# An expert stage in which each pair of experts gathers its own token rows

## The chip, the cores and the metric

The kernel runs on one core of a Trainium2 chip. The metric is device time in microseconds, the median of several executions; the profile is one execution of its own. Engines are named PE (TensorE), DVE (VectorE), ACT (ScalarE), POOL (GpSimd) and SP (SyncE, which here only issues transfers).

## What is computed

Two transformer blocks over 512 tokens of width 1024, all in float32. The first mixes a convolution with latent attention and ends in a mixture of experts; the second has two layers of sliding-window and sparse attention with a dense feed-forward part. The change is in the mixture of experts and in the add behind it:

```
g_idx = top_1(softmax(h @ w_group))                   # 4 groups
e_idx = top_2(softmax(h @ w_expert in that group))    # 8 experts each, 32 in all
gates[token, expert] = g_top * e_top / sum(e_top)     # two experts a token
for e in range(32):
    a = silu(h @ w_gate_e[e]) * (h @ w_up_e[e])       # 1024 -> 256
    y += gates[:, e] * (a @ w_down_e[e])              # 256 -> 1024
x = x + g_f * y
```

h is the second norm of x with scale and shift. Each token goes to two of 32 experts, so there are 1024 (token, expert) rows, 32 an expert on average.

## The kernel before

Everything is written by hand, with a program for each engine and semaphores between them; an engine does its work in the order of its program.

**Routing.** POOL makes ramps and constants (lines 977 to 983), then the rstd of the second norm (987, 988), for which DVE waits at line 1641. PE turns the normed rows (L2145), makes the logits (L2292), and counts with matmuls how many tokens before each chose the same expert (L2300 to L2303). DVE makes prefix sums of the counts, and from them for every row a place in a list sorted by expert. PE turns the places into a list of token numbers with a one-hot product (L2310, "rows"), and in the same way into a list of target rows ("slots"). POOL then gathers all 1024 sorted rows with eight indirect transfers (L993) out of token_rows, a copy of the normed rows in HBM. PE turns them in 64 pieces of 128x128, and ACT (L1210) and DVE (L1780) apply scale and shift as they empty PSUM in 512 columns, into XsT.

**The loop.** The 32 experts go in 16 pairs (EPAIRS). Each expert has a window of 64 columns (HALF) beginning at its first row. DVE copies the two windows of a pair out of XsT into XW (`window`, L1790), two pairs ahead. PE multiplies them with gate and up weights, the experts side by side in PSUM bank b = p % 2 (L2339, 16 matmuls, 32 in the trace); ACT takes SiLU (L1215), DVE the product (L1795), PE turns it (L2327), ACT copies it (L1219), PE makes the down product (L2356) into two banks of bank b's own pair, DVE (L1799) and ACT (L1223) copy a half each to Y, and POOL scatters the rows to expert_rows in HBM (L1002). The sequence on PE is gate/up of p, turn, down of p, gate/up of p + 1.

**The weights.** SP loads them ahead: 2.1 MB of gate and up for an expert into one of five slots (L830), 1.05 MB of down into one of four (L833), each when the product that last used the slot is done (m_gu, m_y).

**The extra steps.** An expert with more than 64 rows needs further windows of 128. How many there are is read from a register, at least one step is run, and here it is one. It stands behind the last pair on all engines, and loads its weights in the same rings.

**Behind the loop.** SP reads expert_rows back (L872), two rows a token. ACT weights one (L1248), DVE the other and adds (L1857), multiplies by g_f (L1858) and adds to x (L1861); then the second block begins with its input projection (L2398 turns, L2410 products with w_in).

## Time and profile before

| | us |
|---|---|
| three runs | 2058.57, 2051.89, 2056.76 |
| median | 2056.76 |
| the profiled execution | 2054.31, its span 2052.5 |
| PE busy in the span | 1844.0 (90%) |
| DVE, ACT, POOL busy | 915.1, 622.2, 162.3 |
| mean DMA rate | 132 GB/s, 270.38 MB |

The page gives a span in 40 slices of 51 us. The expert stage is slices 7 to 13, from 328 us, where the constants of the routing are made, to 650 us, where the rows are read back. The slices show where the transfers are dense; the timelines give start and duration of each instruction, and behind it in brackets how long the engine had been idle and what it waited for. Durations of matmuls overlap a little, since they are pipelined.

### The profile page before, as it was taken

The page shows a single profiled execution, that of the slowest core. Times are in us where ns is not written, and L with a number is a line of the kernel's source. Part 1 is how long each engine was busy: PE and PEld are TensorE (multiplying, and loading weights), DVE is VectorE, ACT ScalarE, POOL GpSimd, SP SyncE. Part 2 cuts the span into 40 slices and gives each one's busy share as a digit, 9 for nine tenths or more (in the row PEclk, how much of TensorE's full clock was granted, in tenths as well). Part 3 has the DMA queues.
Part 4 walks back from the last instruction along what each step waited for, and adds up shares of the span by engine and source line. Part 5 has one row for each costly group of instructions (what it writes and reads, how often), then busy time and mean ns, then how long its engine had stood idle before and what let it go on. Part 6 is the DMA issues. An engine that isn't in the chain of part 4 may idle for free. (4 is left out here: it accounts for less than half of the span.)

```text
span 2052.5 us, 23756 instructions
## 1 busy us (share of the span) xinstructions
PE 1844.0 (90%) x8688; PEld 1262.0 (61%) x8692; DVE 915.1 (45%) x1646; ACT 622.2 (30%) x1121; POOL 162.3 (8%) x239
## 2 busy tenths in 40 slices
PE   4997996587776899999999999988999999999996
PEld 2444644423222556676788878865557678888785
DVE  3787823511102687682322223347866522222234
ACT  2024521110001225742333322223376223333222
POOL 1000000200000242010000000004500100000001
PEclk9999998799888899999999999999999999999998
DMA  9162034499995500032233342250002203334231
GB/s 377 75 246 83 1 126 164 176 420 421 421 422 199 207 1 13 10 119 57 62 102 89 95 143 82 86 196 1 1 22 114 62 23 100 102 94 151 72 93 42
DMA packets 146334, 270.38 MB, mean 132 GB/s; under 512 B 9344, under 2 KB 106624, under 8 KB 132672
## 3 DMA queue, kind: packets, MB, share of 16 engines
q1 hardware_dynamic: 142208, 259.44, 34.9%
q0 software_dynamic: 4032, 9.69, 1.3%
q8 instruction: 58, 0.95, 0.2%
q14 instruction: 36, 0.29, 0.0%
HBM read 260.72 MB, written 13.11 MB: 133 GB/s over the span
## 5 line engine op out<-in xcount | busy, mean ns | idle before, releaser
L278 PE MATMUL bank<-ht_hi,gate_up_hi 128*128 128x512 f32 x704 | 274.1, 389 | 3.1 <-ACT arena L1429 3.1
L280 PE MATMUL bank<-ht_hi,gate_up_lo 128*128 128x512 f32 x704 | 273.9, 389 | 0.0
L279 PE MATMUL bank<-ht_lo,gate_up_hi 128*128 128x512 f32 x704 | 273.9, 389 | 0.0
L2410 PE MATMUL bank<-arena 128*128 128x512 f32 (+3 forms) x640 | 197.1, 467 | 8.2 <-ACT arena L1276 5.6
L2410 PEld LDWEIGHTS bank<-arena 128*128 128x128 f32 x640 | 115.3, 197 | 84.6 <-issue 67.4
L2054 DVE TENSOR_TENSOR arena<-arena,bank 128x512 f32 (+1 forms) x44 | 30.2, 687 | 272.2 <-ACT arena L1295 272.2
L278 PEld LDWEIGHTS bank<-ht_hi,gate_up_hi 128*128 128x128 f32 x704 | 132.1, 188 | 31.3 <-issue 3.9
L280 PEld LDWEIGHTS bank<-ht_hi,gate_up_lo 128*128 128x128 f32 x704 | 132.1, 188 | 27.7
L279 PEld LDWEIGHTS bank<-ht_lo,gate_up_hi 128*128 128x128 f32 x704 | 132.1, 188 | 27.2
L278 PE MATMUL bank<-down_hi,product_hi 128*128 128x512 f32 x352 | 138.2, 393 | 3.5 <-DVE arena L2054 3.5
L280 PE MATMUL bank<-down_hi,product_lo 128*128 128x512 f32 x352 | 138.1, 392 | 0.0
L279 PE MATMUL bank<-down_lo,product_hi 128*128 128x512 f32 x352 | 138.0, 392 | 0.0
L2048 DVE TENSOR_TENSOR gate_up_lo<-gate_up_whole,gate_up_hi 128x2048 fp32r<-128x2048 f32 x44 | 100.9, 2293 | 67.5 <-ACT gate_up_hi L1289 66.9
L2058 DVE TENSOR_TENSOR down_lo<-down_whole,down_hi 128x1024 fp32r<-128x1024 f32 x44 | 53.9, 1225 | 157.7 <-ACT product_hi L1303 157.7
L2339 PE MATMUL bank<-arena 128*64 128x512 f32 x512 | 113.0, 593 | 8.1 <-DMA arena<-w_up_e 4.0
L1301 ACT CAST down_hi<-down_whole 128x1024 fp32r<-128x1024 f32 x44 | 46.2, 1051 | 164.2 <-PE bank L280 164.2
L2356 PE MATMUL bank<-arena 128*64 128x512 f32 x256 | 73.7, 728 | 20.4 <-DMA arena<-w_down_e 16.9
L1514 DVE SCALAR_TENSOR_TENSOR arena<-arena 128x512 f32<-128x512 f32 x120 | 90.0, 750 | 3.3
L2339 PEld LDWEIGHTS bank<-arena 128*64 128x64 f32 x512 | 40.4, 137 | 78.5 <-issue 78.3
L1289 ACT CAST gate_up_hi<-gate_up_whole 128x2048 fp32r<-128x2048 f32 x44 | 84.0, 1908 | 0.2
L2145 PE MATMUL bank<-arena 128*128 128x128 f32 (+1 forms) x332 | 54.1, 318 | 29.9 <-DVE arena L1575 11.8
L1295 ACT ACTIVATE arena<-bank 128x512 f32<-128x512 f32 x44 | 26.3, 598 | 174.4 <-PE bank L280 174.2
(373 smaller groups left out, 2938.0 us busy)
## 6 DMA issues: line engine op xcount, KB each, us to landing
gate_up_whole<-w_gu SPq DMA_DIRECT2D x88, 512.0 KB, 5.1
arena<-w_gate_e SPq DMA_DIRECT2D x33, 1024.0 KB, 20.1
arena<-w_up_e SPq DMA_DIRECT2D x33, 1024.0 KB, 23.4
arena<-w_down_e SPq DMA_DIRECT2D x33, 1024.0 KB, 23.2
down_whole<-w_down SPq DMA_DIRECT2D x44, 512.0 KB, 3.5
arena<-w_ada SPq DMA_DIRECT2D x5, 4096.0 KB, 21.2
arena<-w_in SPq DMA_DIRECT2D x4, 2048.0 KB, 16.0
w_o_whole<-w_o SPq DMA_DIRECT2D x2, 4096.0 KB, 13.1
```

Source lines behind the costliest of these rows:

```text
L278: pe.matmul(ps, xh, wh, start=start, stop=False)
L279: pe.matmul(ps, xh, wl, start=False, stop=False)
L280: return pe.matmul(ps, xl, wh, start=False, stop=stop)
L1289: act.copy(gu_hi[s], gu[s]).then_inc(f_hi, 1)
L1301: act.copy(dn_hi[f % 2], w_dn[:, f % DN_SLOTS])
L1514: ins = dve.scalar_tensor_tensor(DW[:, m], U[:, m, k:k + S], conv_w[:, m, k:k + 1], DW[:, m], ALU.mult, ALU.add)
L2048: dve.tensor_tensor(gu_lo[s], gu[s], gu_hi[s].bitcast(F32), ALU.subtract).then_inc(f_lo, 1)
L2058: dve.tensor_tensor(dn_lo[f % 2], w_dn[:, f % DN_SLOTS], dn_hi[f % 2].bitcast(F32), ALU.subtract)
L2145: ins = pe.transpose(ps[0:x.shape[-1], n * P:(n + 1) * P], x, ident)
L2339: ins = pe.matmul(bank[b][half_rows(h)], XW[b][:, c, half_rows(h)], ring[gu_slot(2 * p + h)][:, :, c], start=c == 0, stop=c == C8 - 1)
L2356: ins = pe.matmul(bank[4 + 2 * b + half][half_rows(h)], AT[:, b, c, half_rows(h)], ring_d[dn_slot(2 * p + h)][:, c, 512 * half:512 * half ...
L2410: ins = pe.matmul(ps[:, 0:b - a], HT[:, c, t * P:(t + 1) * P], w_in2[j][:, c], start=c == 0, stop=c == C8 - 1)
```

## The change

**Places.** There are no sorted rows any more. An expert's slots are fixed, 64 e to 64 e + 63, and one table gives for every slot the token to read, the row to write and the weight of the row (`mark_places`, `take_table`; from_token, to_row, w_slot). The first table, for the 16 pairs, is made before the loop. The counting of extra steps and their table (`extra_rows`) stand on DVE between the first pair's product and the gating of its rows, and their matmuls on PE behind the second pair's gate/up product.

**Rows.** Pair p gathers its own 128 rows with one indirect transfer into G[p % 2], skipping empty slots; POOL issues the gather of p + 1 behind the scatter of p - 1. PE turns them in eight pieces (`turn_rows`, L2340) into banks 6 and 7, ACT and DVE apply scale and shift in four pieces of 128 columns each (`modulate`), into XT. On PE the down product of pair p stands ahead of the turns of pair p + 1. The down product has one pair of banks, 4 and 5, instead of two.

**Weights of the rows.** DVE multiplies the weight into the product (L1765) and g_f into the rows as it empties PSUM (`gate_rows`, both halves; L1771), so that behind the loop only the add is left.

**Slots and extras.** A sixth gate/up slot and a fifth down slot are filled before the loop and then used by the extra steps, which stand before pair 9. POOL makes two more ramps and clears G before the rstd.

```diff
-XCOLS = 2 * S + P
 HALF = P // 2
 EPAIRS = NE // 2
-COLUMNS = 32
-EXTRAS = COLUMNS - EPAIRS
+EXTRAS = NE - EPAIRS
+EXTRA_AT = 9
+XCOLS = EXTRAS + 1
 ARENA = 53200
 CREDIT = 4
-GU_SLOT, DN_RING = [2, 3, 0, 1, 4], 4
-GU_USES_EXTRA, DN_USES_EXTRA = NE // len(GU_SLOT), NE // DN_RING
-GU_AT_EXTRA, DN_AT_EXTRA = (NE - len(GU_SLOT)) // 2, (NE - DN_RING) // 2
+EXTRA_STEPS = 11
+GU_SLOT = [2, 3, 0, 1, 4, 5] + [[2, 3, 0, 1, 4][n % 5] for n in range(NE - 6)]
+DN_SLOT = [0, 1, 2, 3, 4] + [n % 4 for n in range(NE - 5)]
+GU_EXTRA, DN_EXTRA = 5, 4
+ABSENT = 4096
...
+            for e in (0, 1, 4):
+                load_down(e, DN_SLOT[e])
             u1.read(sp, ("mix", T - 1, 1))
-            load_gate_up(2, gu_slot(2))
-            load_gate_up(3, gu_slot(3))
+            load_gate_up(2, GU_SLOT[2])
+            load_gate_up(3, GU_SLOT[3])
             for t in range(T):
                 sp.wait_ge(s_xhat2, t + 1)
                 sp.dma_start(token_rows[t * P:(t + 1) * P], H[:, t]).then_inc(s_saved, 16)
             for e in range(2, 4):
-                load_down(e, dn_slot(e))
-            u1.all_evacuated(sp, [("xsT", g, c) for g in range(2) for c in range(C8)])
-            load_gate_up(4, gu_slot(4))
+                load_down(e, DN_SLOT[e])
+            load_gate_up(4, GU_SLOT[4])
+            sp.wait_ge(s_saved, 16 * T)
+            u1.read(sp, ("logit", T - 1))
+            load_gate_up(5, GU_SLOT[5])
...
-            sp.wait_ge(s_extra, 1)
-            extras = sp.value_load(n_extra[0:1, 0:1], min_val=1, max_val=EXTRAS)
-            with sp.Fori(0, extras) as x:
-                e = sp.value_load(extra_i[0:1, 0, bass.ds(x, 1)], min_val=0, max_val=NE - 1)
-                sp.wait_ge(m_gfree, x + 1)
-                load_gate_up(e, gu_slot(NE))
-                sp.wait_ge(m_dfree, x + 1)
-                load_down(e, dn_slot(NE))
-            sp.wait_ge(m_st[0], 16 * (EPAIRS // 2 + extras))
...
+            own.mark(pool.iota(column_h, [[1, P]], base=0, channel_multiplier=0, allow_small_or_imprecise_dtypes=True))
+            own.mark(pool.iota(slot_h, [[HALF, NE]], base=0, channel_multiplier=0, allow_small_or_imprecise_dtypes=True))
             own.mark(pool.tensor_copy(ones_b, ones))
             own.mark(pool.tensor_copy(before_b, before_me))
+            own.settle()
+            own.mark(pool.tensor_scalar(column_h, column_h, 0.5 - HALF, None, ALU.add))
+            own.mark(pool.tensor_scalar(slot_h, slot_h, 0.5 - HALF, None, ALU.add))
+            for b in range(2):
+                own.mark(pool.memset(G[b], 0.0))
             own.settle()
             pool.sem_inc(s_count, 1)
...
-            u1.evacuated(pool, ("rows",))
-            for g in range(2):
-                for q in range(T):
-                    pool.indirect_dma_start(stage[g][:, q], None, token_rows,
-                                            bass.IndirectOffsetOnAxis(row_ids[:, T * g + q:T * g + q + 1], 0)).then_inc(s_stage1 if g else s_stage, 16)
-
-            u1.evacuated(pool, ("slots",))
-            pool.memset(XsT[:, :, 2 * S:], 0.0).then_inc(s_pad, 1)
-            last_row = pool.to_reg(2 * S - 1)
+            last_row, last_token = pool.to_reg(2 * S - 1), pool.to_reg(S - 1)
+
+            def gather(p):
+
+                if p >= 2:
+                    pool.wait_ge(m_xt, p - 1)
+                pool.indirect_dma_start(G[p % 2], None, token_rows, bass.IndirectOffsetOnAxis(from_token[:, p:p + 1], 0),
+                                        bounds_check=last_token, oob_is_err=False).then_inc(s_g[p % 2], 16)
...
+            pool.wait_ge(s_tokens, 1)
+            gather(0)
+            gather(1)
+            u1.evacuated(pool, ("table",))
+            apart(pool)
             for p in range(EPAIRS):
-                pool.wait_ge(m_ya, p + 1)
-                pool.wait_ge(m_yb, p + 1)
-                pool.indirect_dma_start(expert_rows, bass.IndirectOffsetOnAxis(slots_i[:, p:p + 1], 0), Y[:, p % 2], None,
-                                        bounds_check=last_row, oob_is_err=False).then_inc(m_st[p % 2], 16)
...
+                if p == EXTRA_AT:
+                    pool.wait_ge(s_extra, 2)
+                    apart(pool)
+                    pool.indirect_dma_start(G[2], None, token_rows, bass.IndirectOffsetOnAxis(from_token[:, EPAIRS:EPAIRS + 1], 0),
+                                            bounds_check=last_token, oob_is_err=False).then_inc(s_gx, 16)
+                    scatter(p - 1)
...
+                elif p:
+                    scatter(p - 1)
+                if p + 1 < EPAIRS and p:
+                    gather(p + 1)
+            scatter(EPAIRS - 1)
...
+            def modulate(b):
+
+                for c in range(C8 // 2):
+                    ins = act.activation(XT[b][:, c], bank[6 + c // 4][:, c % 4 * P:(c % 4 + 1) * P], ACT.Identity,
+                                         bias=mod[:, 2, c:c + 1], scale=mod[:, 3, c:c + 1])
+                return ins
+
+            act.wait_ge(m_xt, 1)
+            modulate(0).then_inc(m_xw, 1)
...
+                act.wait_ge(m_gu, p + 1)
                 if p >= 2:
                     act.wait_ge(m_a, p - 1)
-                silu(p, b)
+                silu(b).then_inc(m_silu, 1)
+                act.wait_ge(m_at, p + 1)
                 if p >= 2:
                     act.wait_ge(m_y, p - 1)
-                copy_at(p, b)
-                if p >= 2:
-                    act.wait_ge(m_st[b], 16 * (p // 2))
-                copy_y(p, b)
...
-            def weight_second(t):
-
-                act.wait_ge(s_yin[t], 16)
-                act.activation(Yin[:, t, 1], Yin[:, t, 1], ACT.Copy, scale=wts[:, t, 1:2]).then_inc(s_w1, 1)
-
-            weight_second(0)
-            weight_second(1)
+                copy_at(b).then_inc(m_atc, 1)
+                if p + 1 < EPAIRS:
+                    act.wait_ge(m_xt, p + 2)
+                    modulate(1 - b).then_inc(m_xw, 1)
...
+            def mark_places(n):
+
+                own.settle()
+                own.link(dve.tensor_tensor(place, OHS, tmp32.unsqueeze(1).broadcast_to([P, 2, T, NE]), ALU.mult))
+                own.link(dve.tensor_reduce(dest_k, place.rearrange("p k t e -> p (k t) e"), AX, ALU.add))
+                own.link(dve.tensor_scalar(tile_k, dest_k, 1.0 / P, ROUND, ALU.mult, ALU.add))
+                own.link(dve.tensor_scalar(tile_k, tile_k, -ROUND, None, ALU.add))
+                own.mark(dve.scalar_tensor_tensor(row_k, tile_k, float(-P), dest_k, ALU.mult, ALU.add))
+                tok, ids, w = (tile_hot[:, :, m * n:(m + 1) * n] for m in range(3))
+                own.link(dve.tensor_tensor(tok, wide_k(tile_k, n), column[:, 0:n].unsqueeze(1).broadcast_to([P, 2 * T, n]), ALU.is_equal))
+                own.mark(dve.tensor_tensor(ids, tok, wide_k(row_ids_k, n), ALU.mult))
+                own.link(dve.tensor_tensor(w, tok, wide_k(wts_k, n), ALU.mult))
+                own.mark(dve.tensor_tensor(tok, tok, wide_k(token_k, n), ALU.mult))
+                own.settle()
+                dve.tensor_tensor(row_hot, wide_k(row_k, P), column_h.unsqueeze(1).broadcast_to([P, 2 * T, P]), ALU.is_equal).then_inc(s_marked, 1)
...
+            def modulate(b):
+
+                for c in range(C8 // 2, C8):
+                    ins = dve.tensor_scalar(XT[b][:, c], bank[6 + c // 4][:, c % 4 * P:(c % 4 + 1) * P], mod[:, 3, c:c + 1], mod[:, 2, c:c + 1],
+                                            ALU.mult, ALU.add)
+                return ins
...
+            def gate_rows(b):
+
+                for half in range(2):
+                    cs = slice(512 * half, 512 * half + 512)
+                    ins = dve.tensor_tensor(Y[:, b, cs], bank[4 + half][:], gate_f[:, cs], ALU.mult)
+                return ins
...
+                own.link(dve.tensor_copy(n_extra[:, 0:1], extra_f[:, 0:1]))
+                later = column[:, 0:EXTRAS].unsqueeze(2).broadcast_to([P, EXTRAS, NE])
+                own.mark(dve.tensor_tensor(begun, extra_e.unsqueeze(1).broadcast_to([P, EXTRAS, NE]), later, ALU.is_gt))
+                own.mark(dve.tensor_tensor(here, pre[k].unsqueeze(1).broadcast_to([P, EXTRAS, NE]), later, ALU.is_gt))
                 own.settle()
+                own.link(dve.tensor_tensor(here, here, begun, ALU.subtract))
+                own.link(dve.tensor_tensor(begun, here, slot0.unsqueeze(1).broadcast_to([P, EXTRAS, NE]), ALU.mult))
+                own.link(dve.tensor_reduce(extra_f, begun, AX, ALU.add))
+                own.link(dve.tensor_scalar(extra_f, extra_f, 1.0 / HALF, None, ALU.mult))
+                dve.tensor_copy(extra_i, extra_f).then_inc(s_extra, 1)
+                own.link(dve.tensor_scalar(shift_e, extra_e, float(P), -float(P - 0.5), ALU.mult, ALU.add))
+                own.mark(dve.tensor_scalar(ML, rank, HALF - 0.5, 2.0 * ABSENT, ALU.is_lt, ALU.mult))
+                own.mark(dve.tensor_tensor(tmp32, rank, shift_e.unsqueeze(1).broadcast_to([P, T, NE]), ALU.add))
+                own.settle()
+                own.mark(dve.tensor_tensor(tmp32, tmp32, ML, ALU.add))
+                mark_places(XCOLS)
...
+                product(b, w_slot[:, p:p + 1]).then_inc(m_a, 1)
+                if p == 0:
+                    extra_rows()
+                if p == 1:
+                    dve.wait_ge(s_tab, 1)
+                    own.mark(take_table(bank[2][:, 2 * P:], EPAIRS, XCOLS, own.mark))
+                    own.settle()
+                    dve.sem_inc(s_extra, 1)
+                dve.wait_ge(m_y, p + 1)
                 if p >= 2:
                     dve.wait_ge(m_st[b], 16 * (p // 2))
-                copy_ya(p, b)
...
+                gate_rows(b).then_inc(m_yc, 1)
+                if p + 1 < EPAIRS:
+                    dve.wait_ge(m_xt, p + 2)
+                    modulate(1 - b).then_inc(m_xw, 1)
...
-                own.link(dve.scalar_tensor_tensor(Yin[:, t, 0], Yin[:, t, 0], wts[:, t, 0:1], Yin[:, t, 1], ALU.mult, ALU.add))
-                own.link(dve.tensor_tensor(Yin[:, t, 0], Yin[:, t, 0], gate_f, ALU.mult))
+                own.link(dve.tensor_tensor(Yin[:, t, 0], Yin[:, t, 0], Yin[:, t, 1], ALU.add))
...
+            def turn_rows(rows):
+
+                for c in range(C8):
+                    ins = pe.transpose(bank[6 + c // 4][:, c % 4 * P:(c % 4 + 1) * P], rows[:, c::C8], ident)
+                return ins
...
+                if p == EXTRA_AT:
+                    pe.wait_ge(s_extra, 1)
+                    extras = pe.value_load(n_extra[0:1, 0:1], min_val=1, max_val=EXTRAS)
+                    with pe.Fori(0, extras) as x:
+                        pe.wait_ge(s_gx, 16 * (x + 1))
+                        pe.wait_ge(m_xw, 2 * (p + 1))
+                        pe.wait_ge(m_extra, step(x - 1, EXTRA_STEPS))
+                        turn_rows(G[2]).then_inc(m_extra, 1)
...
+                if p == 1:
+                    pe.wait_ge(s_marked, 2)
+                    pe.wait_ge(m_atc, 1)
+                    table(bank[2][:, 2 * P:], XCOLS).then_inc(s_tab, 1)
...
+                if p + 1 < EPAIRS:
+                    pe.wait_ge(s_g[1 - b], 16 * ((p + 1) // 2 + 1))
+                    turn_rows(G[1 - b]).then_inc(m_xt, 1)
```

The order on POOL before the routing, of the kernel before (IOTA 128x32 to CAST are the ramps and constants, then the rstd, then the eight gathers):

```order
38 L981 IOTA arena 128x128
39 L982 CAST arena<-arena 128x128
40 L983 CAST arena<-arena 128x128
41 L987 TENSOR_SCALAR arena<-arena 128x4
42 L988 TENSOR_TENSOR arena<-arena 128x4
43 L993 DMA arena<-token_rows,arena 128x1024 x8
44 L997 MEMSET arena 128x8x128
```

and of the changed kernel:

```order
40 L987 IOTA arena 128x32
41 L988 CAST arena<-arena 128x128
42 L989 CAST arena<-arena 128x128
43 L991 TENSOR_SCALAR arena<-arena 128x128
44 L992 TENSOR_SCALAR arena<-arena 128x32
45 L994 MEMSET arena 128x1024 x2
46 L998 TENSOR_SCALAR arena<-arena 128x4
47 L999 TENSOR_TENSOR arena<-arena 128x4
48 L1007 DMA arena<-token_rows,arena 128x1024 x2
49 L1013 DMA expert_rows<-arena 1024x1024
50 L1007 DMA arena<-token_rows,arena 128x1024
```

The clears now stand before the rstd (L998, L999), two gathers are left ahead of the loop, and from then on gathers and scatters alternate.

PE from the last table to the second pair, before (L2145 turns the sorted rows, L2339 is gate/up, L2327 the turn of the product, L2356 down):

```order
203 L2310 MATMUL bank<-arena 128x8 x8
204 L2310 MATMUL bank<-arena 128x32 x8
205 L2145 MATMUL bank<-arena 128x128 x64
206 L2339 MATMUL bank<-arena 64x512 x16
207 L2327 MATMUL bank<-arena 128x128 x2
208 L2356 MATMUL bank<-arena 64x512 x8
209 L2339 MATMUL bank<-arena 64x512 x16
210 L2327 MATMUL bank<-arena 128x128 x2
```

and after (L2340 turns a pair's rows, L2386 is gate/up, L2346 the turn of the product, L2405 down, L2326 a place table):

```order
203 L2326 MATMUL bank<-arena 128x48 x8
204 L2340 MATMUL bank<-arena 128x128 x8
205 L2386 MATMUL bank<-arena 64x512 x16
206 L2346 MATMUL bank<-arena 128x128 x2
207 L2405 MATMUL bank<-arena 64x512 x8
208 L2340 MATMUL bank<-arena 128x128 x8
209 L2386 MATMUL bank<-arena 64x512 x16
210 L2326 MATMUL bank<-arena 128x51 x8
211 L2346 MATMUL bank<-arena 128x128 x2
```

Eight turns have come between a down product and the next gate/up product, and a table behind the second gate/up product.

DVE from the end of the extra steps' marking (L1735) through the first pairs, after (L1771 gates rows, L1759 drains turned rows, L1765 is the product, L1739 to L1741 take the table):

```order
296 L1735 TENSOR_TENSOR arena<-arena 128x1024
297 L1771 TENSOR_TENSOR arena<-bank,arena 128x512 x2
298 L1759 TENSOR_SCALAR arena<-bank,arena 128x128 x4
299 L1765 SCALAR_TENSOR_TENSOR arena<-arena,bank 128x256
300 L1739 TENSOR_SCALAR arena<-bank 128x17
301 L1740 TENSOR_SCALAR arena<-bank 128x17
302 L1741 COPY arena<-bank 128x17
303 L1771 TENSOR_TENSOR arena<-bank,arena 128x512 x2
304 L1759 TENSOR_SCALAR arena<-bank,arena 128x128 x4
```

The gating and the draining of a pair stand behind all that `extra_rows` does; before, there were four window copies around the first product, and none of this.

## Rows read from the trace of the kernel before

**Rows 1.** Stretches of the expert loop, the columns in the first line.

```profile
core 0: us, PE busy (x) PEld busy (x) DVE busy (x) ACT busy (x) POOL busy (x), PEclk, DMA share, GB/s
350.00:384.00 34.00, 11.13 (x62) 10.65 (x62) 25.05 (x95) 1.02 (x3) 9.73 (x9) 0.50 0.29 97
395.40:460.00 64.60, 56.72 (x250) 19.13 (x250) 10.01 (x21) 6.13 (x14) 3.98 (x4) 0.97 0.94 389
460.00:603.00 143.00, 112.42 (x456) 40.69 (x456) 18.02 (x37) 12.42 (x28) 8.79 (x9) 0.90 1.01 421
```

**Rows 2.** Waits of 395:650: us in total, times, longest us.

```profile
PE bank L2356 <- DMA arena<-w_down_e: 16.9, 9, 2.4
```

**Rows 3.** Timeline of PE: start, duration, line, operation, [idle before <-releaser].

```profile
395.44 7.09 PE L2339 MATMUL bank<-arena 128*64 128x512 f32 x32 [3.72 <-DVE arena L1790]
403.46 0.50 PE L2327 MATMUL bank<-arena 128*128 128x128 f32 x2 [0.93 <-DVE arena L1795]
...
407.91 7.04 PE L2339 MATMUL bank<-arena 128*64 128x512 f32 x32
...
433.01 7.04 PE L2339 MATMUL bank<-arena 128*64 128x512 f32 x32
...
442.20 3.65 PE L2356 MATMUL bank<-arena 128*64 128x512 f32 x16 [0.52 <-ACT arena L1219]
445.69 7.04 PE L2339 MATMUL bank<-arena 128*64 128x512 f32 x32
...
454.88 5.35 PE L2356 MATMUL bank<-arena 128*64 128x512 f32 x16 [0.52 <-ACT arena L1219]
```

**Rows 4.** Timeline, the extra step at the end of the loop and the reload.

```profile
633.51 7.13 PE L2370 MATMUL bank<-arena 128*128 128x512 f32 x16 [2.74 <-DVE arena L1819]
...
642.75 3.69 PE L2382 MATMUL bank<-arena 128*128 128x512 f32 x8 [0.60 <-ACT arena L1219]
...
650.68 0.33 SPq L872 DMA_DIRECT2D arena<-expert_rows  x1
```

**Rows 5.** Timelines of POOL and PE between 325 and 385 us.

```profile
371.68 1.12 POOL L993 DMA_INDIRECT arena<-token_rows,arena  x1 [40.06 <-DVE arena L1749]
...
382.57 0.98 POOL L997 MEMSET arena<- 128x1024 f32 x1
...
334.53 5.85 PE L2145 MATMUL bank<-arena 128*128 128x128 f32 x32 [7.61 <-DVE arena L1641]
```

**Rows 6.** Timelines of DVE and PE, the place tables.

```profile
359.31 0.28 DVE L1693 COPY arena<-bank 128x128 f32<-128x128 f32 x1
...
374.36 0.69 DVE L1757 TENSOR_TENSOR arena<-arena 128x512 f32<-128x512 f32 x1
...
366.98 3.58 PE L2310 MATMUL bank<-arena 128*128 128x8 f32 x16 [8.10 <-DVE arena L1739]
```

**Rows 7.** Groups by shape (xcount | busy us, mean ns); PE from 666 us.

```profile
L1780 DVE TENSOR_SCALAR arena<-bank,arena 128x512 f32<-128x512 f32 x8 | 6.5, 810 | 4.8 <-PE bank L2145 4.3
...
L1598 DVE TENSOR_TENSOR arena<-bank,arena 128x512 f32<-128x512 f32 x4 | 2.8, 691 | 3.9 <-PE bank L2226 3.8
...
L1173 ACT ACTIVATE arena<-bank,arena 128x128 f32<-128x128 f32 x8 | 3.6, 456 | 2.9 <-DVE arena L1592 2.9
...
666.29 1.79 PE L2398 MATMUL bank<-arena 128*128 128x128 f32 x8 [4.20 <-DVE arena L1851]
670.67 7.30 PE L2410 MATMUL bank<-arena 128*128 128x296 f32 x16 [2.59 <-DMA arena<-w_in]
677.80 1.05 PE L2398 MATMUL bank<-arena 128*128 128x128 f32 x8
```

**Rows 8.** DMA, 460:600 and 371:372.5: queue, issues (median us to landing).

```profile
q0 software_dynamic: 1296, 1.98, 3.8%
...
expert_rows<-arena POOLq DMA_INDIRECT x9, 8.1
...
arena<-token_rows,arena POOLq DMA_INDIRECT x1, 4.4
```

461 lines of the change are left out of this document (197 added, 264 removed).

## The prediction

> **What bounds the kernel now.** I read the page's slices first: the transfers stand at some 421 GB/s over the middle of the expert loop and at nothing just before it. The view by stretches puts numbers to it [rows 1]: until 460 us PE is busy 56.7 of 64.6 us, and from 460 to 603 us the transfer engines are full (1.01) and PE is not. The waits say the same [rows 2]: the down product waits nine times for w_down_e. So the loop has two halves, and the reader should see both in the timeline of PE [rows 3]. In the first a pair costs 12.47 us (395.44 to 407.91) and later 12.68 us (433.01 to 445.69), and the next gate/up product starts without a gap on the down product's end. In the second a pair needs two experts of 3.146 MB and its scattered rows (1.98 MB for nine scatters [rows 8], 0.22 MB each), 6.51 MB, which at 421 GB/s is 15.5 us. PE has about 3 us of slack in each of those pairs. Behind the loop the extra expert runs alone, and the last down product ends at 642.75 + 3.69 = 646.44 us; the reload of the rows is issued at 650.68 us [rows 4]. Ahead of the loop the clock is at half, 1.2 GHz, and PE is busy 11 of 34 us [rows 1]: that is the route stage, a chain over POOL, DVE, PE and a gather.
>
> The change trades a transfer bound for a chain. I follow that chain to the end of the last down product, and compare with 646.44 us.
>
> **1. Before the routing.** POOL gets two more ramps, two more scalings and two clears of 128x1024 ahead of the rstd of the second norm. One such clear took 0.98 us [rows 5], two are 1.96, and I put 0.9 on the four small ones and the settling. All of it is in POOL's order before the rstd for which DVE, and through it PE (7.61 us idle before 334.53), already waits [rows 5]. Nothing hides it: **+2.9 us**, bounds 2.0 and 3.6.
>
> **2. Route to the first product.** Before, DVE reads the ranks at 359.31 and PE starts the first table at 366.98 [rows 6]. The new chain has no prefix sums: two 128-wide operations and an add, a product and a reduction of 256, four tiny ones, four of 128 and one of 1024. A 512-wide one took 0.69 us and a 128-wide one 0.28 [rows 6], so a column costs 1.07 ns and an operation 0.15 us, and the chain with its gaps 4.7 us. So 359.3 + 2.9 + 4.7 = 366.9, the table 3.6 [rows 6], 370.5, and the gather's issue 1.1 us later as now (370.56 to 371.68 [rows 5, 6]): 371.6, at the same time as today. But one gather of one pair is enough: 4.4 us to landing [rows 8], 376.0. Eight turns on a cold PE take 1.79 us [rows 7], then ACT and DVE each drain four 128x128 pieces. ACT's took 0.456 us [rows 7] and overlap a little, so 1.8 us. The first gate/up product starts at **379.7** instead of 395.44: **-15.7 us**. Before, 64 turns ran just ahead of it and it took 7.09 us [rows 3]; now it starts cold. A down product of the same 16 matmuls took 5.35 us after a thin stretch and 3.65 otherwise [rows 3], so a cold start costs at least 1.7. I take **+2.0** here: it ends at 388.8.
>
> **3. The first pair on DVE.** The counting of the extra steps and their place table now stand on DVE between the first pair's product and the gating of its rows, and the second pair's rows are drained behind both (the order shows it). Counting the chain: 17 small operations of 0.15 to 0.25 us, 3.0; five of 512 at 0.72 each, 3.6; six small or 128-wide ones, 1.3; then the marking again, 3.8. That is 11.7 us, bounds 10 and 13. The product ends 0.9 us after the gate/up product (0.93 us of idle in [rows 3]), the gating is two PSUM operations of 0.69 [rows 7], 1.3 with their overlap, the drain 1.5, handovers 0.2. The second gate/up product starts 15.6 us after the end of the first, at **404.4**. In the kernel before it would have been 5.4. PE stands still 9 us of that, so another cold start, **+1.7**. Behind it PE makes the second place table, eight matmuls: 3.6 us cold [rows 6], less when warm, and 1.16 of it lies in an idle that is there anyway; **+1.0**, bounds 0.5 and 2.5.
>
> **4. Every pair.** The order on PE is now gate/up, turn of the product, down, turns of the next pair's rows, gate/up. Nothing lies between the turns and the next gate/up product to cover the drain. After the down product's end DVE gates its rows (1.3 us), and only then drains: TENSOR_SCALAR of 128x512 from PSUM took 0.81 us [rows 7]; 384 columns less at 1.07 ns leave 0.4, and four behind one another 1.45. PE's own turns take 1.05 us warm [rows 7] and lie under the gating; ACT's four end at 1.0 + 1.7 us, no later than DVE. So PE restarts 2.9 us after the down product's end, which overlapped the next product by 0.17 before: a cycle of 12.68 + 0.17 + 2.9 = **15.75 us**. Bounds of the stall: 2.4, if the pieces take 0.26, and 3.4.
>
> The Trainium skill ("VectorE: DVE Perf Modes", section "The TRN2 errata") gives a DVE operation that reads PSUM a fixed part of 120 cycles at 0.96 GHz, an estimate of 0.26 us for a 128-wide piece, and says that many small tiles pay the fixed part each, so one should tile at 512 or more. The trace has 0.81 us for 512 columns where that sum gives 0.66, so it is low here; by it the stall would be 2.4 us and the whole loop some 7 us shorter. The rule speaks against this change, which replaces wide drains by narrow ones.
>
> The clock belongs here too. It was granted at 0.97 while PE idled some 1.7 us a pair, and at 0.90 with the longer waits [rows 1]; each thin stretch that tips it costs 1.7 us (5.35 against 3.65 [rows 3]). Under the transfer bound that was free; on a PE-bound chain it is not. The new cycle has two thin stretches, one around the product's turn and one at the restart. I take one tip in three cycles, **0.6 us** a cycle, bounds 0 and 1.4.
>
> **5. Are the transfers still late?** Per pair 6.29 + 0.22 scattered + 0.22 gathered = 6.73 MB, 16.0 us at 421 GB/s, beside a cycle of 16.35. Six gate/up and five down slots are filled before the loop, the ring is 2 pairs deep, and the extra step gives the transfers another rest. From 388.8 us on some 93 MB are left, 221 us, so they could be done by about 610. They no longer bound.
>
> **6. The gathers.** A pair's gather is issued behind the scatter of the pair two before it: 1.3 us of gating, 0.8 to POOL, 1.0 issue, 0.3, so 3.4 us after the down product. Under full transfers a scatter landed in 8.1 us [rows 8]. It is needed one cycle, 16.2 us, after. Priced at nothing; the slack is 16.2 - 3.4 - 8.1 = 4.7 us.
>
> **7. The extra step** now sits before pair 9: turns 1.05, drain 1.9, the product 7.1, 1.0 + 0.5 + 0.6 for SiLU, product and turn, 3.7 down (as 633.51 to 646.44 [rows 4]), gating 1.4, loop entry and handovers 0.7: **18.0 us**, bounds 16.5 and 21. At the end it cost 15.7. Moving it earns nothing, since the chain, not the loads, is the bound.
>
> **8. The tail.** The last gating is 1.3 instead of 0.69 us: **+0.6**. The weighting by ACT and one DVE pass per tile go, but PE's first projection of the second block waits for w_in at 670.67 [rows 7], a transfer issued after the reload, so they are worth nothing.
>
> **The sum.** 404.4; pair 1 is 15.75 + 1.7 + 1.0 = 18.45, 422.85; thirteen cycles of 16.35 are 212.55, 635.4; the extra 18.0, 653.4; the last pair without a stall 12.85 and 0.4 for the clock, **666.6**. Against 646.44 that is +20.2, with the tail **+20.8 us**. The profiled execution took 2054.31 us (span 2052.5), so its twin would take 2075.1; it lay 2.45 below the median of the three runs, 2056.76, so I predict 2077.6, rounded to **2077 us**. What a measurement of this kernel can tell from no change is about 0.3%, 6.2 us.
>
> **Rivals.** (a) **A light chain**: narrow drains at 0.26 us (-7) and no clock lost in the cycles (-8). +6 us, 2063, on the edge of no change. For it: PE is busy 12.2 of such 15.75 us, 78%, and in the stretch with 0.97 it was hardly more. Against it: the 0.81 and 0.456 rows.
> (b) **The loads still pace the loop** (the other side). If a pair took under 14.9 us, the early start of 15.7 us and the extra in the middle would come through; at a stall of 1.2 us, with the cycle 14.05, it is 14 x 2.3 = 32 us less than forecast, 2045. The place is the restart after the down product. For it: DMA is what waits show today [rows 2]. Against it: the gating alone is 1.3 us in front of DVE's drain.
> (c) **Gathers come late**: same queue as the scatter. If the gather lands 8.1 us after the scatter has landed rather than after its own issue, it comes at 2.1 + 8.1 + 8.1 = 18.3 us against 16.2: 2.1 x 13 = +27, 2104. It decides from 12.8 us between issue and landing.
> (d) That the change doesn't do what it says is ruled out by the order: down does stand before the turns on PE, and the extra before pair 9.
>
> **Numbers.** Forecast 0.58, (a) 0.22, half of it within 0.3%, (c) 0.12, (b) 0.08. Slower 0.80, same 0.12, faster 0.08. The range for 8 in 10 runs from the light chain (2063, and 1 below), 2062, to the forecast with 1.4 us of clock a cycle and a little gather wait, 2096.
>
> **What would show it.** In the profile after: first gate/up product at 380 us and not 395; some 10 us between the first down product and the second gate/up product, ended by DVE; waits of PE for the drain of some 1.9 us times 14; hardly any wait for w_down_e; the transfers' share under 1 throughout; last down product at 667 us. If waits for weights or for token_rows head the list, I am wrong by (b) or (c); if the restart comes under 2 us after the down product, by the drain.

## The result, and the profile after

The changed kernel takes **2067.4 us** in the median (2065.76 to 2071.78), the kernel before 2056.76. The ratio is 1.0058 with an interval of [1.0041, 1.0075], so it is slower, by some 11 us. 2077 was forecast, inside 2062 to 2096. The profiled execution has a span of 2064.0 us. Of all executions behind the numbers below only one was slow, one of the twelve of extra_late (2801.23 us), and its ratio leaves it out.

The start of the loop, timeline of PE of the kernel after (start, duration, line, operation, [idle before <-releaser]). L2386 is the gate/up product, L2405 the down product, L2340 the turns of rows:

```profile
373.74 1.94 PE L2340 MATMUL bank<-arena 128*128 128x128 f32 x8 [4.91 <-DMA arena<-token_rows,arena]
377.32 9.01 PE L2386 MATMUL bank<-arena 128*64 128x512 f32 x32 [1.64 <-issue]
...
388.29 3.65 PE L2405 MATMUL bank<-arena 128*64 128x512 f32 x16 [0.46 <-ACT arena L1245]
...
401.13 9.05 PE L2386 MATMUL bank<-arena 128*64 128x512 f32 x32 [8.10 <-DVE arena L1759]
...
419.18 7.09 PE L2386 MATMUL bank<-arena 128*64 128x512 f32 x32 [1.59 <-ACT arena L1250]
...
434.58 7.09 PE L2386 MATMUL bank<-arena 128*64 128x512 f32 x32 [1.59 <-ACT arena L1250]
```

The first product starts at 377.32 instead of 395.44 [rows 3]. It takes 9.01 us, at a granted clock of 0.78 over it, where the third, the same matmuls, takes 7.09 at 1.00; such a slow product behind an idle stretch is called cold below. The second stands 8.10 us behind DVE, and from 419.18 on a pair costs 15.40 us, the extra step and its neighbours apart. Before it was 12.68 as long as the loads kept up, and 15.8 in the mean of the ten pairs from 460 us on. The last wait of the cycle is put down to ACT. The reader sees why in all engines of one restart of the kernel after:

```profile
447.22 1.17 PE L2340 MATMUL bank<-arena 128*128 128x128 f32 x8
...
447.33 1.29 DVE L1771 TENSOR_TENSOR arena<-bank,arena 128x512 f32<-128x512 f32 x2 [4.72 <-PE bank L2405]
448.42 1.50 ACT L1250 ACTIVATE arena<-bank,arena 128x128 f32<-128x128 f32 x4 [4.84 <-PE bank L2340]
448.54 1.36 DVE L1759 TENSOR_SCALAR arena<-bank,arena 128x128 f32<-128x128 f32 x4
448.90 1.01 POOL L1013 DMA_INDIRECT expert_rows<-arena  x1 [13.08 <-DVE arena L1771]
...
449.98 7.09 PE L2386 MATMUL bank<-arena 128*64 128x512 f32 x32 [1.59 <-ACT arena L1250]
```

PE turns the rows in 1.17 us and then waits 1.59 us for the drain. The gating (L1771) lies beside PE's turns. ACT ends at 449.92 and DVE at 449.90, so this profile alone can't tell which of the two holds PE; drain_first below can. The waits of PE from 375 to 670 us (in total, times, longest) hold no load of weights any more, where w_down_e had 16.9 us in nine [rows 2]:

```profile
PE bank L2386 <- ACT arena L1250: 20.7, 13, 1.6
PE bank L2346 <- DVE arena L1765: 16.1, 16, 1.1
...
PE bank L2386 <- DVE arena L1759: 8.1, 1, 8.1
...
PE bank L2340 <- DMA arena<-token_rows,arena: 4.0, 1, 4.0
```

The stretches of rows 1, of the kernel after:

```profile
core 0: us, PE busy (x) PEld busy (x) DVE busy (x) ACT busy (x) POOL busy (x), PEclk, DMA share, GB/s
...
395.40:460.00 64.60, 49.23 (x230) 18.79 (x232) 15.44 (x40) 7.54 (x20) 8.10 (x8) 0.92 0.84 335
460.00:603.00 143.00, 111.11 (x490) 41.82 (x488) 27.19 (x63) 19.58 (x52) 19.47 (x21) 0.98 0.95 386
```

The last of those wait rows, 4.0 us for token_rows, stands behind the extra step. Timelines of PE and, below, of POOL there (L2365 is the extra's gate/up product, L1036 its scatter, L1038 the gather of the next extra, L1007 the gather of a pair):

```profile
529.99 7.13 PE L2365 MATMUL bank<-arena 128*128 128x512 f32 x16 [1.67 <-ACT arena L1250]
...
544.24 7.09 PE L2386 MATMUL bank<-arena 128*64 128x512 f32 x32 [1.38 <-DVE arena L1771]
...
561.05 1.16 PE L2340 MATMUL bank<-arena 128*128 128x128 f32 x8 [4.05 <-DMA arena<-token_rows,arena]
563.81 9.63 PE L2386 MATMUL bank<-arena 128*64 128x512 f32 x32 [1.59 <-ACT arena L1250]
```

```profile
545.52 1.00 POOL L1036 DMA_INDIRECT expert_rows<-arena  x1 [0.84 <-POOL arena L1033]
546.82 1.04 POOL L1038 DMA_INDIRECT arena<-token_rows,arena  x1 [0.30 <-issue]
552.32 1.00 POOL L1007 DMA_INDIRECT arena<-token_rows,arena  x1 [4.46 <-issue]
```

Inside the extra loop POOL's program waits for its scatter to land (`pool.wait_ge(s_sx, ...)`) before it leaves the loop, and the gather of pair 10 stands in its order behind that; the view shows the wait of 4.46 us without a releaser. A steady pair's gather is issued 0.23 us behind the start of the gate/up product, this one 8.08 us behind it (552.32 less 544.24). PE waits 4.05 us for it, and the product behind that starts cold, 9.63 us for 7.09. The last down product ends at 656.05 us (before: 646.44), and the reload is issued at 660.36 (before: 650.68 [rows 4]): 9.7 of the 11.5 us of span are there. Behind the reload, in stages that the change doesn't touch, the distance at one and the same load is first 8.4 us and later 11.5, so 3.1 us of the span come there, and no run shows from what; these are SP's rows, first of before, then of after:

```profile
817.98 0.35 SPq L900 DMA_DIRECT2D arena<-ln_g  x1
...
1877.89 0.97 SPq L920 DMA_DIRECT2D arena<-ln_g  x1
```

```profile
826.37 0.35 SPq L904 DMA_DIRECT2D arena<-ln_g  x1
...
1889.37 0.73 SPq L924 DMA_DIRECT2D arena<-ln_g  x1
```

### The profile page after: what moved, and what is told of

The parts are those of the page before. It is cut to its first block and busy times, and to the rows that moved or that the text cites. A ratio compares the mean times of both kernels' runs of the same rounds, so it can differ in the third digit from the quotient of the medians.

```text
span 2064.0 us, 23821 instructions
## 1 busy us (share of the span) xinstructions
PE 1845.5 (89%) x8760; PEld 1259.2 (61%) x8764; DVE 919.1 (45%) x1680; ACT 626.7 (30%) x1160; POOL 172.9 (8%) x255
## 5 line engine op out<-in xcount | busy, mean ns | idle before, releaser
L2438 PE MATMUL bank<-arena 128*128 128x512 f32 (+3 forms) x640 | 196.1, 465 | 11.7 <-DMA arena<-w_in 6.2
L2386 PE MATMUL bank<-arena 128*64 128x512 f32 x512 | 119.8, 623 | 31.8 <-ACT arena L1250 20.7
L2386 PEld LDWEIGHTS bank<-arena 128*64 128x64 f32 x512 | 37.1, 143 | 104.4 <-issue 70.7
L1060 POOL TENSOR_SCALAR arena<-arena 128x1 f32<-128x1 f32 x12 | 7.1, 594 | 897.3 <-ACT arena L1286 897.3
L276 PEld LDWEIGHTS bank<-down_hi,product_hi 128*128 128x128 f32 x352 | 66.1, 188 | 19.2 <-issue 4.3
## 6 DMA issues: line engine op xcount, KB each, us to landing
arena<-w_up_e SPq DMA_DIRECT2D x33, 1024.0 KB, 11.5
arena<-w_down_e SPq DMA_DIRECT2D x33, 1024.0 KB, 14.8
```

Source lines behind the costliest of these rows:

```text
L276: pe.matmul(ps, xh, wh, start=start, stop=False)
L2386: ins = pe.matmul(bank[b][half_rows(h)], XT[b][:, c, half_rows(h)], ring[GU_SLOT[2 * p + h]][:, :, c], start=c == 0, stop=c == C8 - 1)
L2438: ins = pe.matmul(ps[:, 0:b - a], HT[:, c, t * P:(t + 1) * P], w_in2[j][:, c], start=c == 0, stop=c == C8 - 1)
```

## The experiments

Two theories stood against one another. **Chain**: PE's restart behind the down product (turns, then drain) sets the cycle, and the transfers no longer do. **Loads**: they still pace the loop, since their share is 1.01 from 475 to 515 us in the kernel after too. Times are compared as ratios to the kernel before on the same chip. In the runs below that was 2053.5 to 2057.03 us.

### Does the chain or do the loads set the cycle? (half_loads_after, half_loads_before)

```diff
                 for k, w in enumerate(("w_gate_e", "w_up_e")):
+                    if k and not (isinstance(e, int) and e < 6):
+                        sp.dma_start(ring[s][:, k, 0:1], i[w][0][bass.ds(e, 1)].rearrange("a (p c) n -> (a p) c n", c=C8)[:, 0:1]).then_inc(s_gu[s], 16)
+                        continue
```

> The kernel after with the up weights of the experts from 6 on (and of the extra step) loaded only in one of their eight rows: 7 of 24 parts of the loads are left out, the output isn't the reference's, every instruction on PE, DVE, ACT and POOL stays. Chain theory (drain and gating between the down product and the next gate/up product set the cycle of 15.40 us): each steady cycle stays 15.40 us; only the late gather behind the extra step, 4.05 us and the cold product after it, may go because transfers are no longer crowded: 2060 to 2067 us. Load theory (full transfers, 1.01 from 475 to 515 us, hold the cycle): cycles fall under 15 us and the time under 2055. Crowding theory (loads slow the drains): cycles fall by some tenths.

> The same loads left out of the kernel before, output not the reference's. If from 460 us on it is bound by transfers, its ten pairs of 15.5 us fall to 12.7 and the time to 2056 - 28 = about 2028 us, and hardly a wait for w_down_e is left. If the pairs were bound by something else it stays near 2056. On the clock: if down products of 5.35 us instead of 3.65 come from the waits for weights, they go with the waits; if they come in a dense cycle as well, some remain in cycles of 12.7 us.

The kernel after with fewer loads took 2060.63 us, ratio 1.0024 [1.0013, 1.0035]. Its share of transfers falls to 0.80 from 460 to 603 us, its cycles stay at 15.40. What it gained is the late gather (no wait for token_rows behind the extra step: PE goes from pair 9 to pair 10 in 15.45 us instead of 19.57) and the cold product behind it. The chain theory holds for the cycle. Its rows, in the middle of the loop:

```profile
466.60 7.09 PE L2389 MATMUL bank<-arena 128*64 128x512 f32 x32 [1.59 <-ACT arena L1253]
...
482.00 7.09 PE L2389 MATMUL bank<-arena 128*64 128x512 f32 x32 [1.59 <-ACT arena L1253]
```

The kernel before with fewer loads took 2035.09 us, ratio 0.9886 [0.9867, 0.9905]: 22 us faster where 28 were expected. Its pairs do fall to 12.68 where no product is slow, and no wait for w_down_e is left. The missing 6 us are slow products: from 460 us on five down products of 5.35 us (8.5 us in all) and an extra product of 8.82 instead of 7.13. That is more than 6, but the ten pairs before took 15.8 us and not the 15.5 of the expectation. With the one at 455.38 the down products of 5.35 stand in six of its pairs, behind the same 0.52 us of idle as the ones of 3.65, here with one of 3.65 between:

```profile
455.38 5.35 PE L2359 MATMUL bank<-arena 128*64 128x512 f32 x16 [0.52 <-ACT arena L1222]
...
469.75 3.65 PE L2359 MATMUL bank<-arena 128*64 128x512 f32 x16 [0.52 <-ACT arena L1222]
...
509.48 5.35 PE L2359 MATMUL bank<-arena 128*64 128x512 f32 x16 [0.52 <-ACT arena L1222]
```

Over the first of them the granted clock is 0.68, over the one of 3.65 it is 1.00. So those products don't come from waits for weights.

### What is in the stall? (drain_first)

```diff
+                if p + 1 < EPAIRS:
+                    dve.wait_ge(m_xt, p + 2)
+                    modulate(1 - b).then_inc(m_xw, 1)
                 dve.wait_ge(m_y, p + 1)
...
                 gate_rows(b).then_inc(m_yc, 1)
-                if p + 1 < EPAIRS:
-                    dve.wait_ge(m_xt, p + 2)
-                    modulate(1 - b).then_inc(m_xw, 1)
```

> The kernel after with one change: on DVE the drain of the next pair's rows stands ahead of the gating of the product; PE's order stays. In the kernel after PE's restart waits 1.59 us for ACT's four pieces (417.62 + 1.50 = 419.12), and DVE ends at the same time (419.11), with the gating lying beside PE's turns. ACT theory (the stall is the turns plus ACT's drain, the gating isn't in it): cycle 15.40 us as before this change, time as after, 2064 to 2069 us. DVE theory of the prediction (gating 1.3 us ahead of the drain makes the stall): the cycle falls by some 1.0 to 1.3 us, the time by 13 to 18, to 2050 to 2054. The scatter is issued 1.4 us later; more late gathers would lengthen it by 4 to 7 us.

2067.09 us, ratio 1.0067 [1.005, 1.0084], as the kernel after. The cycle stays 15.40:

```profile
447.82 1.50 ACT L1250 ACTIVATE arena<-bank,arena 128x128 f32<-128x128 f32 x4 [4.83 <-PE bank L2340]
447.82 1.36 DVE L1759 TENSOR_SCALAR arena<-bank,arena 128x128 f32<-128x128 f32 x4 [5.80 <-PE bank L2340]
449.11 1.28 DVE L1771 TENSOR_TENSOR arena<-bank,arena 128x512 f32<-128x512 f32 x2
...
449.38 7.09 PE L2386 MATMUL bank<-arena 128*64 128x512 f32 x32 [1.59 <-ACT arena L1250]
```

The gating is not in the stall: with it moved behind the drain, PE waits the same 1.59 us for ACT. Here DVE ends at 449.18, 0.14 us ahead of ACT, and PE still starts behind ACT. The stall is PE's own turns (1.17) and ACT's four pieces (1.50). The scatter and with it each gather came later, by 2.4 us against the gate/up product beside it (451.98 less 449.38, where the kernel after has 450.21 less 449.98), not by the 1.4 expected. That already made PE wait for rows in five places, in four pairs by 0.3 to 0.7 us and ahead of the extra's own turns by 2.08 us, where it stood 1.79 in the kernel after anyway. The slack of 4.7 us that the prediction gave the gathers was some 2 in those pairs. The total as it was is then in part chance: in this profile the gather of pair 10 is in time and its product warm (6.7 us less), the second gate/up product starts 1.2 us earlier, and the late rows with three slow products (9.64, 8.91, 8.78) give it back. The evidence on the stall is the cycle, not the total.

### Undo the order on PE (turns_first)

```diff
+                if p + 1 < EPAIRS:
+                    pe.wait_ge(s_g[1 - b], 16 * ((p + 1) // 2 + 1))
+                    turn_rows(G[1 - b]).then_inc(m_xt, 1)
                 pe.wait_ge(m_a, p + 1)
...
                 ins.then_inc(m_y, 1)
-                if p + 1 < EPAIRS:
-                    pe.wait_ge(s_g[1 - b], 16 * ((p + 1) // 2 + 1))
-                    turn_rows(G[1 - b]).then_inc(m_xt, 1)
```

with the drain ahead of the gating on DVE, as above, and the gather of p + 1 ahead of the scatter of p - 1 on POOL.

> The changed kernel with the new order undone: on PE the turns of the next pair's rows stand between gate/up and the turn of the product, on DVE the drain stands behind the product and ahead of the gating (in pair 0 ahead of the counting too), and POOL issues a gather ahead of the scatter. Chain theory: the stall of 2.67 us at each restart (1.17 turns and 1.59 idle) goes, since drain and gating lie under the down and gate/up products: a cycle of 12.9 instead of 15.40 as long as the loads keep up; from then on the loads pace it, 16.0 us a pair, so waits for w_down_e and w_up_e come back. By bytes the loads end near 607, the last down product near 620, the whole some 2031, below the kernel before. Rival: the stall has another cause (a bank, a buffer, the gather), the cycle stays at 15.4 and the whole at 2067 less the 6.6 of the late gather.

**2035.18 us**, ratio 0.9904 [0.9886, 0.9922]: 32 us faster than the change as it is, and 20 faster than the kernel before. PE's turns fill the idle before the turn of the product, and the drain lies under the down product. The timeline of PE, with no idle between down and gate/up product:

```profile
455.12 1.16 PE L2340 MATMUL bank<-arena 128*128 128x128 f32 x8
456.19 0.51 PE L2346 MATMUL bank<-arena 128*128 128x128 f32 x2
457.15 3.65 PE L2408 MATMUL bank<-arena 128*64 128x512 f32 x16 [0.46 <-ACT arena L1245]
460.64 7.04 PE L2386 MATMUL bank<-arena 128*64 128x512 f32 x32
```

The cycle is 12.49 us there. Of its three moves the one on DVE brought nothing by itself (drain_first); the one on POOL wasn't tried alone. Then the loads are the bound again; its waits of 375:640:

```profile
PE bank L2408 <- DMA arena<-w_down_e: 12.8, 6, 3.2
...
PE bank L2386 <- DMA arena<-w_up_e: 6.8, 5, 2.4
```

### Where turns_first ends (half_loads_turns, turns_best)

turns_first with the loads left out as above:

> turns_first with the up weights of the experts from 6 on (and of the extra step) loaded only in one of their eight rows; output not the reference's. If the loads pace turns_first in its second half (12.8 us of waits for w_down_e, 6.8 for w_up_e, and 1.7 and 3.0 us of slow products behind two of them), the waits and those go: -23 us, 2012 us. If a chain stands right behind the loads, less than 10 us are gained, 2025 or more. On the clock: the dense cycle of 12.68 us in the kernel before lost 1.7 us in six of thirteen pairs without any wait for weights; if a dense cycle as such does that, some products of 5.35 us stand here too; if it is that cycle's two idles of 1.16 and 0.52 us together, none.

2014.7 us, ratio 0.9812 [0.9793, 0.9831], some 20 us below turns_first, where 23 were expected: the loads do bound it, and without them its cycles are 12.49 us from 437 us on, the two beside the extra step apart. turns_best adds the edits of count_later and clear_later (below) to turns_first.

> turns_first with the clears behind the rstd and with the counting of the extras behind the drain of pair 1's rows, their marks in pair 1, their table at pair 2. Chain alone would give -1 and -3 (in turns_first the second gate/up product already starts early, the third 18.5 us after it instead of 12.7). If from 475 us on the loads pace this version (six waits for w_down_e of 3.2 us, five for w_up_e of 2.4), most of that is eaten: 2032 to 2035 us. If it is still a chain: 2029 to 2031.

2038.84 us, ratio 0.9924 [0.9909, 0.9939], which is no better than turns_first. Its third gate/up product started at 405.49, 4.6 us earlier than in turns_first, and its last down product ended at 627.81 where turns_first's ended at 627.14. Its waits for weights are as long as in turns_first (14.5 us for w_down_e in seven and 5.5 for w_up_e, against 12.8 and 6.8). What took the 4.6 us back is the table, now in pair 2 (1.6), and more slow products behind waits for weights, four down products of 5.35 us and a gate/up product of 8.78 (8.5 us over the usual, 4.6 in turns_first). That the loads alone would have taken it is likely and not shown.

### The first pair (count_later)

The counting stands behind the drain of pair 1's rows, the marks in pair 1 and the table at pair 2:

```diff
                 product(b, w_slot[:, p:p + 1]).then_inc(m_a, 1)
-                if p == 0:
-                    extra_rows()
-                if p == 1:
+                if p == 2:
                     dve.wait_ge(s_tab, 1)
...
+                if p == 0:
+                    extra_rows()
+                if p == 1:
+                    extra_marks()
```

> The changed kernel with the counting of extra steps moved on DVE from behind the first pair's product to behind the second pair's drain, its marking to behind the third pair's drain, and the table's matmuls on PE behind the third pair's gate/up product. Chain theory: the second gate/up product starts 2.7 us after the first down product's end (391.94 + 2.7 = 394.6) instead of at 401.13, and takes 7.09 instead of 9.05 us: 8.4 us off the chain, last down product at 647.6, the whole some 2059. Load theory: under 2 us of it are seen at the end.

2051.28 us, ratio 0.998 [0.9969, 0.9992]: 16 us below the kernel after, where 8 were expected, and just below the kernel before. From the first gate/up product to the third it took 32.78 us instead of 41.86, and the table then cost 0.7 in pair 2: 8.4 us, as expected. The rest of the gain is the gather behind the extra step, which came 0.96 us late in this profile instead of 4.05, with no cold product behind it, less 1.6 for a slow product in the extra step (8.68 us instead of 7.13). That part hangs on when the extra's scatter lands (POOL waited 2.86 us for it before it issued the gather, 4.46 in the kernel after), and I don't count it as an effect of the edit. From the first gate/up product to the end of the last down product it is 266.3 us instead of 278.7, 12.4 less; the other 4 us of the medians lie outside this stretch and stay unexplained.

### The gathers around the extra step (gather_early, gather_between, extra_late)

gather_early moves the gather of pair 10 ahead of the extra's own gather on POOL, gather_between puts it behind that and the scatter of pair 8 but ahead of the loop, extra_late sets EXTRA_AT = 15, where no pair's gather follows.

```diff
                 if p == EXTRA_AT:
+                    gather(p + 1)
                     pool.wait_ge(s_extra, 2)
...
-                if p + 1 < EPAIRS and p:
+                if p + 1 < EPAIRS and p and p != EXTRA_AT:
                     gather(p + 1)
```

> The changed kernel with one edit: on POOL the gather for pair 10 is issued before the scatter of pair 8 and before the extra step, not behind it. Chain theory (PE's own serial chain sets the time, each us taken off it comes off the whole): in the changed kernel PE waited 4.05 us for token_rows ahead of pair 10's turns, and the gate/up product behind it took 9.63 us instead of 7.09. Both go: the last down product ends 6.6 us earlier than 656.05, at 649.4, and the whole is 6.6 us shorter, some 2061. Load theory (the transfers pace the loop): the wait moves to the weights and the last down product still ends near 656. Clock theory apart: if 9.63 came from a late transfer and not from the clock after an idle stretch, it stays over 9 with the wait gone.

> The kernel after with the gather of pair 10 behind the scatter of pair 8 and ahead of the extra loop on POOL. Moving it ahead of the extra's own gather (gather_early) only moved the wait: the extra's turns then waited 3.40 us. Queue theory: here neither waits, since the extra's gather keeps its place and the other has 30 us: from pair 8's to pair 10's gate/up product 32.7 + 15.4 = 48 us instead of 52.2, time 2062 to 2063. If slower clock near the extra step (9.7 to 10 us instead of 7.1 for its product in three other kernels) takes it back, 50 to 51 us there and 2064 or so.

> The kernel after with its extra step before pair 15 instead of before pair 9. Chain theory: the extra step costs the same 17.3 us wherever it stands, but no gather follows it (the last pair's was issued before), so the 4.05 us wait for token_rows and the cold product behind it, 6.7 us together, go: 2061 us. If the rest that it gives the transfers in the middle mattered (loads still pace), waits for weights appear in pairs 10 to 14 and it is no faster or slower than 2067.

gather_early: 2062.71 us, 1.0031 [1.0018, 1.0044]. The time is as expected, but the profile says that the reason is not. The wait moved to the extra's own rows, now third in POOL's queue, and a cold product came with it:

```profile
530.82 1.97 PE L2341 MATMUL bank<-arena 128*128 128x128 f32 x8 [3.40 <-DMA arena<-token_rows,arena]
534.45 10.03 PE L2366 MATMUL bank<-arena 128*128 128x512 f32 x16 [1.67 <-ACT arena L1251]
```

From the first gate/up product to the end of the last down product it took 277.5 us, the kernel after 278.7, so this profile shows 1.2 of the 5 us between the medians. gather_between: 2058.98 us, 1.0017 [1.0005, 1.003], 274.6 us for the same stretch. No wait for token_rows is left in it. That is 4.1 of the 6.7 expected; the medians differ by 8.4, more than expected, and the rest lies outside the stretch. What took 2.6 us back is the same scatter by another way: DVE's product of pair 9 writes a buffer of the extra step and waits until POOL (L1042) says that the extra's scatter has landed, so PE stood 1 us longer and one down product took 5.35:

```profile
551.06 0.48 DVE L1766 SCALAR_TENSOR_TENSOR arena<-arena,bank 128x256 f32<-128x256 f32 x1 [8.60 <-POOLq L1042]
...
551.60 0.51 PE L2347 MATMUL bank<-arena 128*128 128x128 f32 x2 [1.99 <-DVE arena L1766]
```

extra_late: 2060.4 us, 1.0011 [0.9999, 1.0023], 271.8 us for the stretch: 7.0 less than the kernel after, 6.7 expected. All its pairs from the third on are 15.40 us, none waits for weights. So moving the extra step into the middle brought nothing, and cost the late gather.

How late that gather is changes from profile to profile. With the kernel after's order on POOL around the extra step, POOL's wait ahead of it was 4.46 us in the kernel after, 2.86 in count_later, 1.66 in clear_later and 1.28 in drain_first and, with fewer loads, half_loads_after, and PE waited 4.05, 0.96, 0, 0 and 0 us. So 6.7 us is its price in one profile. That it costs something in the medians too is shown by gather_between and extra_late, whose intervals lie below that of the kernel after.

### The clears (clear_later)

```diff
             own.settle()
+            pool.wait_ge(s_ss2, T)
+            own.link(pool.tensor_scalar(rstd, ss, 1.0 / D, EPS, ALU.mult, ALU.add))
+            pool.tensor_tensor(rstd, rstd, half_neg, ALU.pow).then_inc(s_rstd2, 1)
             own.mark(pool.tensor_scalar(column_h, column_h, 0.5 - HALF, None, ALU.add))
...
-            pool.wait_ge(s_ss2, T)
-            own.link(pool.tensor_scalar(rstd, ss, 1.0 / D, EPS, ALU.mult, ALU.add))
-            pool.tensor_tensor(rstd, rstd, half_neg, ALU.pow).then_inc(s_rstd2, 1)
```

> The changed kernel with POOL's two clears and two scalings behind the rstd of the second norm instead of ahead of it. Chain theory: DVE's wait for the rstd, 5.88 us in the changed kernel, becomes 3.2, and everything behind it comes 2.7 us earlier; the whole 2.7 us shorter, some 2064.7. Rival: PE's counting matmuls wait for POOL's constants instead, or the gathers do, and nothing is gained.

2062.47 us, 1.0032 [1.0019, 1.0045]. DVE's scaling, in the kernel after, and then in clear_later with POOL's clears beside it:

```profile
332.88 2.74 DVE L1664 TENSOR_SCALAR arena<-arena 128x1024 f32<-128x1024 f32 x4 [5.88 <-POOL arena L999]
```

```profile
330.44 4.66 DVE L1664 TENSOR_SCALAR arena<-arena 128x1024 f32<-128x1024 f32 x4 [3.02 <-POOL arena L993]
...
332.04 1.85 POOL L997 MEMSET arena<- 128x1024 f32 x2
```

The wait fell by 2.86 us, but the four scalings took 1.92 longer. Ahead of PE's turns some 1.0 us was gained (9.66 us of idle instead of 10.61), not 2.9. Most of the 4.9 us between the medians is not the edit: the late gather is absent from this profile (6.7 us), and three products are slower in it, 9.68, 9.39 and 9.69 us instead of 9.01, 9.05 and 7.13 (3.6 us). The Trainium skill ("SBUF — State Buffer", section "Who interferes with whom") says that a DVE instruction in a 2-port mode and GpSimd share one pair of ports, and that one blocks the other. The trace agrees in kind, with 2.74 against 4.66 us; that these scalings run in such a mode no run here shows.

## Why the prediction was right or wrong

The sign and the side were right (slower, +20 forecast, +11 measured), by the mechanism named in part 4. By its own steps, at the end of the last down product 666.6 us were forecast and 656.05 came:

- **Part 1**, +2.9: PE stood idle 10.61 us ahead of the product that follows rstd, 7.61 before [rows 5], +3.0; and DVE waited 5.88 us for rstd, 3.02 in clear_later. Right. The whole stage lay 1.9 us earlier in the profile after (PE's matmuls ahead of it end at 325.06 and not at 326.92); no run shows why.
- **Part 2**, 379.7: it was 377.32, of which those 1.9 us. The cold start was put at 2.0 and took 1.9 (9.01 against 7.09).
- **Part 3**, the second product 15.6 us after the end of the first, at 404.4: 14.8, at 401.13. The counting took 11.4 us (387.18 to 398.6), 11.7 forecast. count_later shows that 8.4 us of it were only a matter of place.
- **Part 4**, 15.75 us: 15.40. The size was right but its reasoning was half wrong. "After the down product's end DVE gates its rows (1.3 us), and only then drains" is true and doesn't matter, as drain_first shows: ACT, which the prediction only put down as "no later than DVE", ends at the same time as DVE (0.02 us later), and alone holds PE as long. 13 cycles at 0.35 are 4.6 us too many.
- **The clock in part 4**, "I take one tip in three cycles, 0.6 us a cycle", is the mis-sized term: in the steady cycles not one product was slow, so 13 x 0.6 = 7.8 us were missing. The step that failed is "each thin stretch that tips it": it ties slow products to idle of PE. half_loads_before has six down products of 5.35 us in cycles that are otherwise 12.68 us, with PE busy for 88% of 460:603; the kernel after has none in its steady cycles of 15.40, where PE is busy for 80%. Cold starts after long idle are another matter and were sized right: 9.01 and 9.05 after 4.9 and 8.1 us, forecast 1.7 to 2.0 over 7.09; the one behind the late gather, which wasn't forecast, cost 2.5.
- **Part 5**: right. No wait for weights was left, and half_loads_after shows that they don't bound, though the share of transfers was 0.95 over the stretch. "The transfers' share under 1 throughout" was wrong: it was 1.01 from 475 to 515 us, while no product waited for weights.
- **Part 6**, priced at nothing with a slack of 4.7 us: right for thirteen of fourteen gathers, wrong for the one behind the extra step, which costs 4.2 us of wait and 2.5 of a cold product, +6.7 in this profile. Part 7 saw "loop entry and handovers" and not that POOL leaves the loop only when a scatter has landed. It is rival (c) in one pair, by another way: its program holds POOL, not the queue. Three experiments give it as 4.1 (gather_between, net of what came back), 7.0 (extra_late) and 6.6 us (half_loads_after: 272.1 instead of 278.7). drain_first shows that in several pairs the slack was some 2, not 4.7.
- **Part 7**, 18.0: 17.26 (544.24 less 511.58 is 32.66, less a cycle of 15.40). "Moving it earns nothing" was right.
- **Part 8**, +0.6: +0.1 (4.31 us from the last down product to the reload, 4.24 before). PE waited 6.16 us for w_in at 679.42, where it waited 2.59 before. At that product the distance is 8.75 us (679.42 less 670.67), 0.9 less than at the reload, so the shorter work was worth 0.9 us and not nothing.

The sum: -2.4 (part 2), -0.9 (3), -0.4 (the second pair), -4.6 and -7.8 (4), -0.7 (7), +6.7 (6) and -0.5 (the last pair) are -10.6 us, the 666.6 that became 656.05. That the forecast of +20 came within 10 us is in part luck: 17.3 us of it were too much, and 6.7 us that it had at nothing made up for some. The sign rests on those 6.7 us too. Without the late gather the change is at the edge of no change, 1.0017 [1.0005, 1.003] in gather_between and 1.0011 [0.9999, 1.0023] in extra_late, and with the counting elsewhere it is at 0.998 (count_later). So the chain of part 4 is shown; that by itself it outweighs the early start is not.

Of the rivals (a), the light chain, had half of the truth: no clock lost. It took its narrow drains from a price that isn't there. The Trainium skill ("VectorE: DVE Perf Modes", section "The TRN2 errata") gives (120 + 128) cycles at 0.96 GHz for a 128-wide piece from PSUM on VectorE and (172 + 128) cycles at 1.2 GHz on ScalarE, estimates of 0.26 and 0.25 us. The trace has 1.36 and 1.50 for four, 0.34 and 0.375 each, and the measurement decides. Rival (b), 2045 us and less if the restart were short, is what turns_first then was: with no stall at all the early start came through, to 2035, until the loads bound.

## What to carry to other kernels

When a kernel leaves a transfer bound, ask what now stands between the end of one long product and the start of the next. Work that must be drained before the next product (turns of rows) belongs ahead of the last product of the cycle, so that the drain lies under it; here that order, with its drains and gathers moved along, turned +0.6% into -1.0%. Count the waits inside a loop on a DMA queue's engine as waits of all that stands behind the loop. And before you price a move, see who ends last: an operation in front of a drain costs nothing if another engine drains until the same time.
